# Gated delta rule, one iteration of the pipelined loop: v's turns go where the first state read stood, the read goes behind the second update, and two exponentials of the chunk decays go behind a copy

## What is computed

```python
gc = jnp.cumsum(g.reshape(b, h, n, CHUNK), axis=-1)
diff = gc[..., :, None] - gc[..., None, :]
decay = jnp.exp(jnp.where(tril_incl, diff, -jnp.inf))
kb = kc * bc[..., None]
a_mat = jnp.where(tril_strict, jnp.einsum('bhnid,bhnjd->bhnij', kb, kc) * decay, 0.0)
l_mat = a_mat + jnp.eye(CHUNK, dtype=a_mat.dtype)
u = lax.linalg.triangular_solve(l_mat, vc * bc[..., None], left_side=True, lower=True, unit_diagonal=True)
w = lax.linalg.triangular_solve(l_mat, kb * jnp.exp(gc)[..., None], left_side=True, lower=True, unit_diagonal=True)
attn_intra = jnp.einsum('bhnid,bhnjd->bhnij', qc, kc) * decay

def step(state, inp):
    a_i, qd_i, kt_i, u_i, w_i, gl_i = inp
    v_new = u_i - jnp.einsum('bhck,bhkv->bhcv', w_i, state)
    o_i = jnp.einsum('bhck,bhkv->bhcv', qd_i, state) + jnp.einsum('bhij,bhjv->bhiv', a_i, v_new)
    state = state * gl_i[..., None, None] + jnp.einsum('bhck,bhcv->bhkv', kt_i, v_new)
    return state, o_i
```

## Time and profile before

| what | value |
|---|---|
| median of 3 runs (lowest, highest) | 1531.7 us (1531.52, 1535.36) |
| the profiled execution: its time, its span | 1534.37 us, 1532.6 us |
| PE busy in the span | 1470.8 us, 96% |
| DVE, ACT, POOL busy | 800.2, 626.7, 411.6 us |
| mean granted TensorE clock | 0.989 of full speed |
| the delta loop | from about 1160 to 1298 us of the span |

### The profile page before, as it was taken

One profiled execution on the slowest core, in us unless ns is written; L12 is line 12 of the kernel. 1 busy time (PEld: TensorE's weight loads), 2 busy tenths in 40 slices (PEclk: granted clock), 3 DMA queues, 4 the chain that ended last, 5 costly groups with the idle time before them and its releaser, 6 DMA issues.

```text
span 1532.6 us, 31219 instructions
## 1 busy us (share of the span) xinstructions
PE 1470.8 (96%) x12826; PEld 1287.1 (84%) x12826; DVE 800.2 (52%) x1493; ACT 626.7 (41%) x1297; POOL 411.6 (27%) x509
## 2 busy tenths in 40 slices
PE   6999999989999999998999999999998998999998
PEld 5999998868888777776799999888897887788887
DVE  5248311158888767644330616433433776888531
ACT  5322121047777567643232211343324553777310
POOL 0112132100000166632212211222114775344420
PEclk9999999999999999999999999999997999999999
DMA  7413322000000113147321435533111111212332
GB/s 241 65 49 102 98 77 90 1 1 1 1 1 1 51 62 76 52 142 168 124 56 28 60 76 90 81 57 55 28 43 56 30 38 57 98 59 75 107 124 83
DMA packets 84468, 103.55 MB, mean 68 GB/s; under 512 B 25375, under 2 KB 68543, under 8 KB 84328
## 3 DMA queue, kind: packets, MB, share of 16 engines
q1 hardware_dynamic: 84328, 101.56, 25.8%
HBM read 78.40 MB, written 23.12 MB: 66 GB/s over the span
## 4 chain that ended last, share of the span: by engine, by line
PE 51%; DVE 4%; ACT 2%; issue 1%; DMA 1%; POOL 0%; SPq 0%; DVEq 0%; ACTq 0%
PE s_ps L362 23%; PE s_ps L1291 10%; PE s_ps L2746 2%; PE s_ps L2732 2%; PE s_ps L2721 1%; PE s_ps L2162 1%; DMA qT<-s_gate 1%; PE s_ps L1117 1%; PE s_ps L1098 1%; PE s_ps L2105 1%; PE s_ps L2709 1%; PE s_ps L2120 1%; PE s_ps L2722 1%; PE s_ps L1277 1%; PE s_ps L1670 1%
## 5 line engine op out<-in xcount | busy, mean ns | idle before, releaser
L328 POOL TENSOR_TENSOR p_w_lo<-p_w_raw,p_w_hi 128x2048 fp32r<-128x2048 f32 (+1 forms) x27 | 125.4, 4646 | 526.2 <-ACT p_w_hi L312 526.2
L362 PE MATMUL s_ps<-p_w_hi,w_out_hi 128*128 128x256 f32 (+1 forms) x640 | 181.9, 284 | 0.1
L362 PE MATMUL s_ps<-p_w_hi,w_out_lo 128*128 128x256 f32 (+1 forms) x640 | 179.7, 281 | 0.0
L362 PE MATMUL s_ps<-p_w_lo,w_out_hi 128*128 128x256 f32 (+1 forms) x640 | 179.5, 281 | 0.0
L362 PE MATMUL f_ps<-p_w_hi,hT_hi 128*128 128x256 f32 x576 | 164.0, 285 | 3.0 <-DVE p_w_lo L322 3.0
L362 PE MATMUL f_ps<-p_w_lo,hT_hi 128*128 128x256 f32 x576 | 162.9, 283 | 0.0
L362 PE MATMUL f_ps<-p_w_hi,hT_lo 128*128 128x256 f32 x576 | 162.8, 283 | 0.0
L362 PEld LDWEIGHTS s_ps<-p_w_hi,w_out_hi 128*128 128x128 f32 x640 | 120.6, 188 | 0.9 <-issue 0.6
L362 PEld LDWEIGHTS s_ps<-p_w_lo,w_out_hi 128*128 128x128 f32 x640 | 120.8, 189 | 0.0
L362 PEld LDWEIGHTS s_ps<-p_w_hi,w_out_lo 128*128 128x128 f32 x640 | 120.6, 188 | 0.0
L362 PEld LDWEIGHTS f_ps<-p_w_hi,hT_hi 128*128 128x128 f32 x576 | 109.3, 190 | 3.3 <-issue 3.3
(11 more groups left out here) (296 smaller groups left out, 3627.5 us busy)
## 6 DMA issues: line engine op xcount, KB each, us to landing
p_w_raw<-w_in SPq DMA_DIRECT2D x27, 1024.0 KB, 8.4
s_gate<-p_spill SPq DMA_DIRECT2D x48, 128.0 KB, 1.8
kbT<-x SPq DMA_DIRECT2D x8, 512.0 KB, 7.0
b_w_raw<-w_out SPq DMA_DIRECT2D x8, 512.0 KB, 4.3
qT<-s_gate SPq DMA_DIRECT2D x8, 512.0 KB, 5.7
qT<-x SPq DMA_DIRECT2D x8, 512.0 KB, 3.7
s_x<-qT SPq DMA_DIRECT2D x8, 512.0 KB, 3.2
c_table<-s_line SPq DMA_DIRECT2D x8, 512.0 KB, 3.7
```

The costliest lines, as they stand in the source:

```text
L328: ops.tensor_tensor(self.w_lo[:, c % 2, :, 0:w], self.raw[:, :, 0:w], self.w_hi[:, c % 2, :, 0:w].bitcast(F32), ALU.subtract).then_inc(sel ...
L362: last = self.nc.tensor.matmul(out, lhs, rhs, start=(kt == 0 and i == 0), stop=(kt == KT - 1 and i == 2))
```

## The change

In `order`, the calls after `z` of level 2 are put in another sequence, and ACT's `decays` is cut in two: the four Relu stay, the Exp and the two small Exp become a step of their own, `decays_end`, called behind `z` of level 2. On PE, DVE and POOL `decays_end` is empty. No instruction is added, removed or resized.

```diff
         if v:
             inv.z(i - 1, 2)
-        recur(rec.read, 0)
+        if f:
+            front.decays_end(i)
+        if f:
+            front.values(i)
         if v:
             inv.update(i - 1, 2)
+        recur(rec.read, 0)
         if f:
             front.khat_turn(i)
-            front.values(i)
         if i + 1 < N:
             front.ends(i + 1)
...
                 for h in range(H4):
                     last = nc.scalar.activation(dec[:, 0, h, :], gch[:, t % 2, h, :], ACT.Relu, bias=minus_gc[:, t, h:h + 1])
                 last.then_inc(s["dec_cut"], 1)
+
+            @staticmethod
+            def decays_end(t):
                 act.wait_ge(s["dec_cut"], 2 * t + 1)
                 nc.scalar.activation(dec[:, 0, :, :], dec[:, 0, :, :], ACT.Exp, scale=-1.0)
                 act.wait_ge(s["ends_ready"], t + 1)
```

More of the change, by code:

```diff
@@ L2059, in decays @@
             def decays(t):
+                pass
+            @staticmethod
+            def decays_end(t):
                 pass
```

## The result

| | kernel before | changed kernel |
|---|---|---|
| median of 9 runs each (lowest, highest) | 1531.7 us (1528.9, 1535.43) | 1522.96 us (1518.72, 1527.81) |
| ratio, 95% interval | | 0.9947 [0.993, 0.9964] |
| profiled execution: time, span, granted clock | 1534.37, 1532.6 us, 0.989 | 1527.81, 1526.0 us, 0.991 |

The change makes the kernel 8.7 us faster by the medians. The profiled execution of the changed kernel is the slowest of its nine runs, so its trace shows less of a gain than the medians: 1534.37 - 1527.81 = 6.6 us. The interval of the ratio reaches from 5.5 to 10.7 us.

A forecast was written before the change was run, and what follows sets the result against it. PE was taken to bound the kernel, chiefly through the first state read's wait for ACT's copy of w. 4.3 + 0.35 + 0 = 4.6 us off the median 1531.7 gave 1527.1, rounded to 1527.0; range 1523.8 to 1530.6.

The forecast's parts named there:

- The mechanism of iterations 2 to 7: First state read no longer waits for ACT's copy of w, v's turns cover the second Z's copy: 0.71 us each, 4.3.
- Iteration 8: Last iteration, without a front: second update waits 0.47 for the Z copy; taken as 0, with 0.4 us either way.
- iteration 1's term: No read, PE at half clock: v's turns fill the second update's wait of 0.47; 0.26 to 0.46, taken as 0.35 us.
- rival B: Filling iteration 1's pause brings PE's full clock back some five groups earlier: 2.3 us more, 1524.8; chance 0.17.
- two pauses like the one filled: Argument against rival B: in iteration 1 the third and fourth Z copies still have nothing beside them on PE.
- The range's upper end: 1530.6 us, described as C with half a microsecond more given back.
- C: `d_vnew` or POOL's stretch comes 0.7 later than reckoned, so half the gain is given back: 2.4 us, 1529.3; chance 0.20.
- D: DVE's `d_tl` is held by POOL to its stretch's end, delaying `d_S`: 3.4 us slower, 1535.1, or 1538.1; chance 0.08.
- The reserve at POOL's first mask: POOL's idle time before the first mask of `d_Al`, 1.82 before, was to shrink to 0.35 us, hiding POOL's delay.

The follow-up runs named there:

- rest_only: Kernel before with the whole change in iterations 2 to 8 alone, the old order in 0 and 1; 1525.68 us against 1530.0.
- warm_before: Kernel before plus unread matmuls on PE: 12 in each of iteration 0's two long waits, 3 before each of iteration 1's five updates; 1529.72 us against 1532.08.
- warm_after: Changed kernel plus unread matmuls on PE: 12 in each of iteration 0's two long waits, 3 before updates 1, 3, 4, 5 of iteration 1; 1525.15 us against 1532.08.
- after_again: The changed kernel itself, unaltered, measured a second time; 1522.74 us against 1531.75 for the kernel before, ratio 0.9941.
- the two kinds of kernel in the last table: Four kernels with v's turns in iteration 1's pause and no fillers, against three with it open: loop's start 21.8 against 23.8 us on the mean.
- fill_one: Kernel before plus three unread matmuls on PE ahead of the second update of iteration 1, nothing moved; 1527.4 us against 1532.08, ratio 0.9982.
- The two halves apart: Kernel before with the whole change in iterations 0 and 1 alone, 1527.91 us, and in iterations 2 to 8 alone, 1525.68; both against 1530.0.
- fill_rest: Changed kernel plus three unread matmuls on PE ahead of each of updates 1, 3, 4 and 5 of iteration 1; 1525.31 us against 1532.08 for the kernel before.

## Why the prediction was wrong

**The mechanism of iterations 2 to 7 was right, step by step.** The read's wait is gone, v's turns cover the second Z's copy, and the gain is 0.71 in the iterations 2 and 3 and up to 0.77 in the later ones, for a forecast of 0.71 (bounds 0.63 to 0.80). What my replay had too long was the read: the keys' turns follow it after 0.99, not 1.07. The sum of this term, 4.3, was measured as 4.3 (`rest_only`, medians), 4.2 to 4.6 (`warm_before` less `warm_after`) and 4.5 between the starts of `apply_u` (92.00 before, 87.54 in `after_again`). Its source is mostly ACT: the three exponentials ahead of the copy of w. Iteration 8 was taken as nothing with 0.4 either way; from its `apply_u` to the next it takes 13.69 (13.86 in `after_again`), before 13.61, so it gives 0.1 to 0.25 back.

**The step that failed is iteration 1's term, mis-sized: 0.35, in the prediction's words "as the clock comes back at a time of its own, it is worth 0.26 (the same work at full clock) to 0.46".** It is about 2 to 3: 2.6 between the two traces, 1.9 between the two kinds of kernel in the last table (1.5 to 2.6 at a like fall of the clock), 2.8 by the ratio of `fill_one`, whose interval alone would allow 0.6 to 4.9. The clock does not come back at a time of its own; in the traces it was back beside the second update or ahead of it wherever the pause was filled, and 3.7 to 8.2 us behind it where the pause was open, and a group of PE that then runs at full clock is shorter by some 0.45 (the turns of the normalised keys 0.66 in place of 1.12). That is rival B, which had 0.17 and a price of 2.3 on top of the 0.35. Its total with the forecast, 4.6 + 2.3 = 6.9 from the median, would have been 1524.8. What I held against it, that two pauses like the one filled remain in iteration 1, miscounted (four remain, 0.46 to 0.47 each, at the updates 1, 3, 4 and 5) and was no reason: the clock came back with these four open. Nor is one rise alone in the trace of the kernel before: its granted clock is also down to 0.80 and 0.86 in the two windows of 10 us from 530 and to 0.66 in the one from 720, and up again behind them. Both bounds of this term, 0.26 and 0.46, price the pause and take the clock's return as given, so they did not bound it.

**What is left**, 8.7 less about 7, is what puts the median below the range: with 4.3 and 2.6 alone it would be 1524.8, inside. It lies within what the runs of one kernel differ by. The nine runs of the changed kernel go from 1518.72 at a clock of 0.998 to 1527.81 at 0.991; half-clock stretches also come and go at other places of the span (from 530 to 550 us the clock is 0.83 in the trace of the changed kernel and 1.00 in that of `after_again`). The second measurement gave 9.0 (`after_again`). The two halves apart give 2.1 + 4.3 = 6.4 by their medians, and their intervals reach over the difference; I don't assign it to a part.

**The range's upper end** does not follow from its own words: C with half a microsecond more given back is 1529.3 + 0.5 = 1529.8, not 1530.6. The miss lies at the other end, so nothing hangs on it.

**C did not occur.** The reserve at POOL's first mask is 0.29, of 0.35 forecast, and in the iterations 2 to 7 the first write follows the third z without a wait for `d_vnew`.

**D did not occur.** `d_tl` took 0.63 to 0.70 in four iterations, where it ended with the POOL operation it met, and 0.16 in iteration 2, and `d_S` waited for PE. That agrees with the Trainium skill ("SBUF — State Buffer", section "Who interferes with whom"), by which a DVE instruction with two SBUF inputs and a GpSimd instruction that reads SBUF exclude each other for a whole instruction. Who wins between two queued ones the page leaves open; in these four iterations it was DVE.

**Still open** is where the half-clock stretch of the loop's start begins. It is 17.1, 10.2 or 6.8 us long in executions of nearly the same program, and in part of the same one: 10.2 and 6.8 are both the changed kernel, by a fall 2.5 us later and a return about 1 sooner. The pause is shown to move the stretch's end; what moves its beginning, and where exactly the end falls when the pause is open, no run here settles.

## What to carry to other kernels

If PE runs a stretch at half clock, price a pause there by what the stretch costs and not by the pause's own length: 0.47 us filled with work that had to be done anyway was worth some 2 to 3 us here. Where an engine copies for the bottleneck, look first at what stands in its queue ahead of the copy: three exponentials behind it instead of ahead gave most of the steady gain, and no matmul had to move for that.

## What was not expected of the hardware

The run-to-run spread of this kernel goes with the clock: between the extremes of the nine runs of the changed kernel each 0.001 of the mean granted clock came with about 1.3 us (1527.81 - 1518.72 = 9.1 over 0.998 - 0.991 = 0.007). So a comparison of medians also compares which half-clock stretches the runs caught, and a change that looks like a reordering can act through them.

In iteration 7 of the changed kernel's trace PE stands still with nothing that the profile shows to wait for. The chain that ended last:

```profile
1264.98 0.62 PE s_ps L2097 x16
1265.60 0.88 issue
1266.48 0.51 PE s_ps L2112 x10
```

It takes 0.7 of that iteration's gain (15.28 between the starts of `apply_u`). In the 5 us before it the DMA engines were busy:

```profile
1260.00:1265.00 5.00, 4.91 (x106) 4.48 (x108) 2.59 (x6) 3.31 (x10) 4.71 (x5) 1.00 0.88 333
```

A load of 2 MB was landing (9.7 us from issue to landing). In `after_again`, the same program, that iteration takes 14.6, although its load takes 9.5 us as well. In `rest_only` and `fill_rest` it takes 14.59. So it is no price of the change; its cause was not tried and stays open.
